# Griffin-style block with 64 experts on one core: the experts' sums kept with channels on partitions, and a narrower overlap of the two half groups

## The reference, cut to what matters

```python
s = sigmoid(xt @ router_w)                      # 512 x 64
idx = top_k(s + router_bias, 6)                 # 6 experts of 64 for each token
w = s[idx] / sum(s[idx]) * 2.5
y = sum over the 6 of w_e * ((silu(xt @ gate_e) * (xt @ up_e)) @ down_e)   # 1024 -> 256 -> 1024
y = y + ((silu(xt @ ws_gate) * (xt @ ws_up)) @ ws_down)                    # shared expert
out = layer_norm(2 ** 0.25 * xt + y) * g + b
```

## Time and profile before

| what | before |
|---|---|
| time of the profiled execution | 1144.19 us |
| its span, first to last instruction | 1142.2 us |
| median of three runs | 1144.53 us |
| TensorE busy (PE) | 1109.3 us, 97% |
| VectorE busy (DVE) | 723.1 us, 63% |
| ScalarE busy (ACT) | 445.4 us, 39% |
| GpSimd busy (POOL) | 210.3 us, 18% |
| read from HBM over the span | 287.62 MB |
| mean granted TensorE clock | 0.997 |

### The profile page before, as it was taken

One profiled execution on the slowest core, in us unless ns is written; L12 is line 12 of the kernel. 1 busy time (PEld: TensorE's weight loads), 2 busy tenths in 40 slices (PEclk: granted clock), 3 DMA queues, 4 the chain that ended last, 5 costly groups with the idle time before them and its releaser, 6 DMA issues.

```text
span 1142.2 us, 19416 instructions
## 1 busy us (share of the span) xinstructions
PE 1109.3 (97%) x7184; PEld 690.4 (60%) x7184; DVE 723.1 (63%) x1298; ACT 445.4 (39%) x696; POOL 210.3 (18%) x117
## 2 busy tenths in 40 slices
PE   5999999999999999999989999999999999999996
PEld 4889888888888888656534444444444444444443
DVE  7868585858585868685634555555555555555556
ACT  6766665766666656402002112221121122212214
POOL 1443333424243424400010000000000000000000
PEclk9999999999999999999999999999999999999998
DMA  6121212122121303149389999999999999999971
GB/s 241 43 111 42 112 44 110 55 101 78 75 95 60 119 35 134 51 174 376 142 343 419 419 420 421 420 420 419 420 420 420 417 416 416 409 419 415 410 319 78
DMA packets 48323, 286.70 MB, mean 251 GB/s; under 512 B 8994, under 2 KB 10530, under 8 KB 16528
## 3 DMA queue, kind: packets, MB, share of 16 engines
q1 hardware_dynamic: 43088, 272.96, 58.8%
q0 software_dynamic: 5184, 12.98, 2.9%
HBM read 287.62 MB, written 4.19 MB: 255 GB/s over the span
## 4 chain that ended last, share of the span: by engine, by line
PE 52%; DVE 2%; ACT 1%; DMA 1%; issue 0%; POOLq 0%; DVEq 0%
PE pair L1441 22%; PE pair L1504 11%; PE pair L1494 9%; PE pair L935 3%; PE pair L1104 2%; PE pair L186 1%; PE pair L188 1%; DMA xg<-h_rows,idx 1%; PE pair L1452 1%; DVE acc L1648 0%; ACT first L1570 0%; PE pair L1097 0%; DVE table L1326 0%; PE pair L898 0%; PE pair L1118 0%
## 5 line engine op out<-in xcount | busy, mean ns | idle before, releaser
L395 PE MATMUL pair<-hT,w_parts 128*128 128x264 f32 (+1 forms) x2112 | 378.5, 338 | 0.9 <-DVE hT L666 0.5
L395 PEld LDWEIGHTS pair<-hT,w_parts 128*128 128x128 f32 x2112 | 319.7, 189 | 46.5 <-issue 3.8
L242 POOL TENSOR_TENSOR w_parts<-w_raw,w_parts 128x1024 fp32r<-128x1024 f32 x66 | 163.5, 2479 | 295.5 <-ACT w_parts L236 282.1
L1593 DVE TENSOR_TENSOR acc<-acc,pair 128x512 f32<-128x512 f32 x272 | 165.6, 681 | 38.6 <-PE pair L1494 38.6
L1441 PE MATMUL pair<-raw,xgT 128*64 128x512 f32 x768 | 170.3, 595 | 0.1
L927 POOL DMA_INDIRECT xg<-h_rows,idx x36 | 35.9, 997 | 529.9 <-DVE idx L921 461.3
L1441 PEld LDWEIGHTS pair<-raw,xgT 128*64 128x64 f32 x768 | 53.2, 137 | 116.2 <-issue 116.2
L1553 ACT ACTIVATE y_hi<-pair,small 128x512 fp32r<-128x512 f32 x70 | 48.2, 688 | 192.0 <-PE pair L1504 192.0
L1584 DVE TENSOR_TENSOR act_a<-act_s,pair 128x256 f32<-128x256 f32 x35 | 14.8, 422 | 167.9 <-ACT act_s L1546 167.9
L1546 ACT ACTIVATE act_s<-pair 128x256 f32<-128x256 f32 x35 | 13.4, 384 | 224.7 <-PE pair L1441 224.7
L1504 PE MATMUL pair<-raw,aT 128*32 128x512 f32 x768 | 87.4, 595 | 0.0
(11 more groups left out here) (302 smaller groups left out, 1335.0 us busy)
## 6 DMA issues: line engine op xcount, KB each, us to landing
raw<-in_w_gate_up SPq DMA_DIRECT2D x96, 1024.0 KB
raw<-in_w_down SPq DMA_DIRECT2D x48, 1024.0 KB
first<-in_w_gate_up SPq DMA_DIRECT2D x44, 1024.0 KB
w_raw<-in_w_in SPq DMA_DIRECT2D x36, 1024.0 KB, 6.6
first<-in_w_down SPq DMA_DIRECT2D x22, 1024.0 KB
xin<-in_x SPq DMA_DIRECT2D x4, 512.0 KB, 5.5
ws_gu<-in_ws_gate_up SPq DMA_DIRECT2D x1, 2048.0 KB, 7.6
h_rows<-acc SPq DMA_DIRECT2D x4, 512.0 KB, 20.2
```

What stands on the lines that cost most here:

```text
L242: pool.tensor_tensor(w[:, n % PARTS, 1], w_raw[:, n // 2, n % 2], w[:, n % PARTS, 0].bitcast(F32), ALU.subtract).then_inc(sem("w_lo_ready" ...
L395: last = pe.matmul(o, w[:, n % PARTS, pw, k * P:(k + 1) * P], hT[ph][:, k, of], start=(k == 0 and m == 0), stop=(k == KB - 1 and m == 2))
L1593: v.tensor_tensor(part, part, SUM[g], ALU.add).then_inc(sem("sum_free"), 1)
```

## The change

The sums are kept turned, as `accT`: channels on partitions (channel 8c + k in plane k), 512 tokens along a row. It lies where `acc` lay.

- Scatter: for each of eight channel planes the weights are 128 channels of y (every eighth) and ST's columns move: 288 for the low slots (tokens 0 to 287), 288 for the high slots (tokens 224 to 511). Low slots of one plane and high slots of the next run side by side, then the other way round. The rule for items follows: tokens under 288 may stand low, tokens from 224 high. EXTRA is 90, so tables have 154 items.
- The look-up of pair p + 3 goes ahead of the scatter, on TensorE and on VectorE. `down` waits for the first two additions.
- The routing's 0/1 tables (`ones_b`, `before_b`, `chosen`) are bf16; the table keeps three columns of weights, and the two columns of token numbers are written once into the three buffers `table_now`.
- The shared expert's down product makes the turned result (weights `ws_dn` at a stride of eight) in eight steps; the residual is taken from `h1T`.
- SPq: the first gate-up chunks of third 2 are issued last, behind `shared_taken`, since they lie over `h1T`.
- End: eight products with the identity turn each tile back, y moves with a stride of eight, VectorE reads PSUM with a stride of 128 and writes rows into `raw`.

The diff, cut to its core:

```diff
-EXTRA = 2 * P * TOP_K // HALF + (T - 2 * P) * TOP_K // SLOTS
+LOW_END, HIGH_AT = 288, 224
+EXTRA = 2 * HIGH_AT * TOP_K // HALF + (LOW_END - HIGH_AT) * TOP_K // SLOTS
...
-DOWN_BANK = (4, 2, 6, 4)
+DOWN_BANK = (4, 5, 2, 3, 6, 7, 4, 5)
...
-        self.SUM = tuple(banks[n] for n in (4, 5, 6, 7, 1, 2, 3, 0))
+        self.SUM = tuple(banks[n] for n in (4, 5, 1, 7, 6, 2, 3, 0))
...
         sp.wait_ge(sem("shared_up_done"), 4)
+        bring(2, 1, 2)
+        sp.wait_ge(sem("shared_done"), KB)
+        bring(2, 0, 2)
+        sp.wait_ge(sem("shared_taken"), KB)
         for u in range(PAIR):
             bring(2, u, 0)
-        bring(2, 1, 2)
-        sp.wait_ge(sem("shared_done"), TT)
-        bring(2, 0, 2)
...
-            for n in range(2):
-                for j in range(2):
-                    last = pe.matmul(banks[DOWN_BANK[t] + n][:, :], aT[:, j, t * P:(t + 1) * P],
-                                     ws_dn[:, j, n * 512:(n + 1) * 512], start=(j == 0), stop=(j == 1))
+            for j in range(2):
+                last = pe.matmul(banks[DOWN_BANK[k]][:, :], ws_dn[:, j, k::KB], aT[:, j], start=(j == 0), stop=(j == 1))
...
+        pe.wait_ge(sem("pool_step"), BF16_READY)
         for n, of in numbers:
-            for t in of:
-                last = pe.matmul(TOT[:, n * E:(n + 1) * E], ones[:], chosen[:, t, 0], start=(t == of[0]), stop=(t == of[-1]))
+            for t, rows in of:
+                last = pe.matmul(TOT[:, n * E:(n + 1) * E], ones_b[rows], chosen[rows, t, 0], start=(t == 0),
+                                 stop=(t == of[-1][0]))
...
         for m in range(2):
-            st.add(v.tensor_copy(table[:, 0:ITEMS, :, 3 + m],
-                                 tok[:, :, m].rearrange("p (i t) -> p i t", i=1).broadcast_to([P, ITEMS, TT])))
+            st.add(v.tensor_copy(pairs.all_now[:, :, :, :, PARTS_W + m].rearrange("p b u t -> p (b u) t"),
+                                 tok[:, :, m].rearrange("p (i t) -> p i t", i=1).broadcast_to([P, THIRDS * PAIR, TT])))
...
-        for t in range(TT):
-            v.wait_ge(sem("shared_done"), t + 1)
-            v.scalar_tensor_tensor(acc[:, t], acc[:, t], ALPHA, pair[DOWN_BANK[t] // 2][:, :], ALU.mult, ALU.add)\
+        for k in range(KB):
+            v.wait_ge(sem("shared_done"), k + 1)
+            v.scalar_tensor_tensor(accT[:, k], h1T[:, k], ALPHA, banks[DOWN_BANK[k]][:, :], ALU.mult, ALU.add)\
              .then_inc(sem("shared_taken"), 1)
...
+    SIDES = ((LOW, slice(0, LOW_END)), (HIGH, slice(HIGH_AT, T)))
...
+                for k in range(KB):
...
+                    pe.matmul(o[k // 4][:, k % 4 * P:(k % 4 + 1) * P], accT[:, k, rows], ident[:], start=(k % 4 == 0),
+                              stop=False, skip_group_check=True)
...
+                        last = pe.matmul(o[m].rearrange("p (k c) -> p k c", k=KB // 2), ST[b][:, rows],
+                                         part[:].rearrange("p (c k) -> p k c", k=KB)[:, m * KB // 2:(m + 1) * KB // 2],
+                                         start=False, stop=(part is y_lo), skip_group_check=True)
...
+            def add_in(g, turn):
+                for part in (y_hi, y_lo):
+                    for i in range(2):
+                        of, cols = SIDES[(turn + i) % 2]
+                        last = pe.matmul(SUM[g + i][:, cols], part[of, g + i::KB], ST[b][of, cols],
+                                         start=(turn == 0 and part is y_hi), stop=(turn == 1 and part is y_lo),
+                                         skip_group_check=True)
+                return last
+
+            def first_half(g):
                 if g == SHARED:
 
+                    pe.wait_ge(sem("look_free"), p + THIRDS + 1)
                     pe.wait_ge(sem("xgT_ready"), 2 * p + 4)
...
                 if g == LAST:
 
                     pe.wait_ge(sem("aT_ready"), p + 1)
...
+                add_in(g, 0).then_inc(sem("half_done"), 1)
+
+            def second_half(g):
+
+                pe.wait_ge(sem("half_done"), HALVES * p - HALVES + g // 2 + 1)
+                add_in(g, 1).then_inc(sem("sum_done"), 2)
+
+            first_half(0)
+            first_half(2)
+            second_half(0)
+            first_half(4)
+            second_half(2)
+            first_half(6)
+            second_half(4)
+            second_half(6)
...
             turn_a(p)
+            pairs.look_up(pe, p + 3, b)
             scatter(p, (b + 2) % THIRDS)
 
-            pe.wait_ge(sem("sum_free"), ADDS * p + LOOK_AT + 1)
-            pairs.look_up(pe, p + 3, b)
+            pe.wait_ge(sem("sum_free"), ADDS * p + 2)
 
             down(p, b, turn)
...
-            part = acc[:, t, m * 512:(m + 1) * 512]
-            v.tensor_tensor(part, part, SUM[g], ALU.add).then_inc(sem("sum_free"), 1)
+            v.tensor_tensor(accT[:, g], accT[:, g], SUM[g], ALU.add).then_inc(sem("sum_free"), 1)
...
             weigh(p, b)
+            look(p, b)
             add_up(p)
-            look_and_part(p, b)
+            part_y(p)
...
-                rows = acc[:, TILES[t], part]
-                st(v.scalar_tensor_tensor(rows, LAST_AT[t][:, part], neg_mean[:, col], g2[:, part], ALU.add, ALU.mult))
+                rows, of_c = done[t][:, part], slice(part.start // KB, part.stop // KB)
+                st(v.scalar_tensor_tensor(by_k(rows), LAST_AT[t][:, :].rearrange("p (k c) -> p c k", k=KB)[:, of_c],
+                                          neg_mean[:, col], by_k(g2[:, part]), ALU.add, ALU.mult))
```

More of the change, by code:

```diff
@@ L145, in program @@
         mem["ones"] = sb("ones", [P, P])
+        mem["acc_at"] = top[0]
         mem["acc"] = sb("acc", [P, TT, D])
+        mem["accT"] = sb("accT", [P, KB, T], at=mem["acc_at"])
         raw_at = top[0]
@@ L844, in __init__ @@
         thirds = range(THIRDS)
[L846 removed]
+        now = self.all_now = mem["table_now"]
         self.table_now = [now[:, b] for b in thirds]
@@ L924, in gather @@
         pool.wait_ge(self.sem("idx_ready"), p + 1)
-        pool.sem_inc(self.sem("gather_begun"), 1)
+        pool.sem_inc(self.sem("pool_step"), 1)
         pool.wait_ge(self.sem("h1_stored"), 16 * TT)
@@ L953, in out_and_route @@
     ident, ones, acc, merged, raw = (mem[n] for n in ("ident", "ones", "acc", "merged", "raw"))
-    h1_rows, table, slot_of, iota = (mem[n] for n in ("h1_rows", "table", "slot_of", "iota"))
+    h1_rows, table, slot_of, iota, accT = (mem[n] for n in ("h1_rows", "table", "slot_of", "iota", "accT"))
     place = top[0]
@@ L1026, in out_and_route @@
     TOT = banks[1][:, TT * E:(TT + 3) * E]
-    numbers = ((0, (0, 1, 2)), (1, (TT - 1,)), (2, (0,)))
+    numbers = [(n, [(t, slice(0, min(P, end - P * t))) for t in range(TT) if end > P * t])
+               for n, end in enumerate((LOW_END, T, HIGH_AT))]
     ROW = 2 * ITEMS
@@ L1359, in _ @@
         pool.wait_ge(sem("pool_step"), 2 * PAIR + 1)
+        pool.memset(ones_b[:], 1.0).then_inc(sem("pool_step"), 1)
+        pool.wait_ge(sem("pool_step"), 2 * PAIR + 2)
+        pool.wait_ge(sem("route_here"), 16 * 9)
+        pool.tensor_copy(before_b[:], before[:]).then_inc(sem("pool_step"), 1)
+        pool.wait_ge(sem("pool_step"), BF16_READY)
         pool.wait_ge(sem("shared_up_done"), 4)
@@ L1392, in experts @@
     parts = lambda t: (slice(0, D),) if t < TT - 1 else (slice(0, D // 2), slice(D // 2, D))
+    by_k = lambda row: row.rearrange("p (c k) -> p c k", k=KB)
+    done = [mem["raw"][:, t // 2, t % 2 * D:(t % 2 + 1) * D] for t in range(TT)]
     @block.sync
@@ L1421, in _ @@
                 sp.wait_ge(sem("out_ready"), i + 1 + (part.start > 0))
-                sp.dma_start(out[t * P:(t + 1) * P, part], acc[:, t, part]).then_inc(sem("stored"), 16)
+                sp.dma_start(out[t * P:(t + 1) * P, part], done[t][:, part]).then_inc(sem("stored"), 16)
         sp.wait_ge(sem("stored"), 16 * (TT + 1))
@@ L1461, in finish @@
             pe.wait_ge(sem("xgT_ready"), 2 * p + 2)
-            for i, t in enumerate(TILES):
-                o = [LAST_AT[i][:, m * 512:(m + 1) * 512] for m in range(2)]
-                for m in range(2):
-                    if i == TT - 1 and m == 0:
+            for t in TILES:
+                o = [LAST_AT[t][:, m * 512:(m + 1) * 512] for m in range(2)]
+                rows = slice(t * P, (t + 1) * P)
+                for k in range(KB):
+                    if t == TT - 1 and k == 0:
                         pe.wait_ge(sem("y_ready"), 2 * p)
-                    pe.matmul(o[m], ident[:], acc[:, t, m * 512:(m + 1) * 512], start=True, stop=False)
-                if i == 0:
+                    pe.matmul(o[k // 4][:, k % 4 * P:(k % 4 + 1) * P], accT[:, k, rows], ident[:], start=(k % 4 == 0),
+                              stop=False, skip_group_check=True)
+                if t == 0:
                     pe.wait_ge(sem("ST_ready"), p)
@@ L1480, in scatter @@
             pe.wait_ge(sem("y_ready"), 2 * p)
-            for g in range(0, ADDS, 2):
-                now = SUMS[g:g + 2]
+            def add_in(g, turn):
```

(16 more changed lines are left out.)

81 lines of the change are left out of this document (44 added, 37 removed).

## The result

The changed kernel takes **1175.78 us** (median of four runs, 1174.22 to 1176.94) against 1144.76 for the kernel before beside it: ratio **1.0275**, interval 1.0251 to 1.0298. It is 31 us slower. The forecast was 1145.5 in a range of 1139 to 1154; the result lies where the first rival, "slower, by strides", put it: 1175 us at a chance of 8%.

The account below looks back on a forecast made before the run. TensorE and the DMA stream were taken to end together in the experts' stage. Pair 34 -1.7, scatter and order -0.4, tail +2.9 and +0.5 sum to +1.3 us on 1144.19: 1145.5 us, range 1139 to 1154.

Parts of the forecast that it names:

- the first rival: Scatter weight loads slow at a stride of eight words, +0.85 us for each of 34 pairs: 1175 us, chance 8%.
- The step that failed: Scatter on TensorE: 16 steps at 0.133 us plus 0.3 for switching array tiling, 2.4 us, nothing added for strides.
- The bound that stood in the same paragraph: Upper end for the scatter: 3.9 us if the strided weight loads ran at half their rate.
- All three signs of being wrong: Scatter over 3.1 us, gate-up never waiting for a weight, or last VectorE passes still at 1.28 us.
- The two bounds: Experts' stage: TensorE at 15.23 us a pair and the DMA stream at 16.0 to 16.3 end together; 0.5 us room.
- The stream's start: Third pair's first chunks are issued later, behind the last shared addition, so the DMA stream is delayed: +1.9 us.
- The gathers: Over 32 gathers the fullest block of eight slots has 249 rows, not 256: -1.0 us on the DMA stream.
- The routing and the first gather: Before the pairs: cheaper bf16 routing instructions, -1.4 us; shorter TensorE wait for the first gather, -0.7 us.
- The tail: Last normalization: VectorE's strided PSUM pass at 2.0 us a tile, +2.9; TensorE's products moving strided y, +0.5 us.
- the penalty for a new line of PSUM: Skill's rule cited for the stride rival: accesses each falling in a new 8-byte line of PSUM run slower.
- The rival that it doesn't do what it says: Scatter's half-height products of different columns not running side by side, 16 steps becoming 32; counted with the first rival.
- The rival of a faster kernel, where the stream is no bound: Experts' stage: DMA engines have room, so TensorE's 10 us and the start's 2 come through: 1135 us, chance 6%.

Follow-up runs that it names:

- Half loads: Only half the columns of each down chunk loaded from pair 3 on: in the contiguous version 1127.48 us, in the kernel before 1144.42 us.
- the contiguous version: Changed kernel with the experts' down-weight columns laid out in eight planes of 128, so y is read without a stride: 1146.15 us, ratio 0.9999.

## Why the prediction was wrong, and where it was right

**The step that failed** is the scatter's: "The nearest row for these is the turning of x, which loads weights of that same stride and takes 1.17 us for eight, 0.146 each with its start; so nothing is added." It made 2.4 us; measured 4.09. The row was that of transposes, whose loads are of another kind, and no contiguous row was set beside it to tell whether the stride cost anything in it; the same trace had one (L1452, 140 ns for 195). So the remark that these rows "do not show it for weight loads" was a misreading too. The bound that stood in the same paragraph, 3.9 us for loads at half their rate, was the right one, and the rival's condition (a step over 0.17 us) was met with 0.241. All three signs of being wrong that the prediction names came: a scatter over 3.1 us, a gate-up that never waits for a weight, and VectorE's last passes still at 1.28 us. The rival's own sum, +0.85 us a pair and 1175 us, was right to 0.05 and 1 us; only its chance was wrong.

**The two bounds** were read rightly. Half loads show that the kernel before has 0.44 us from the stream, for which the prediction took 0.5. In the contiguous version, which has the loads that the prediction assumed, the forecast's picture comes out: a step of 0.131 for 0.133, a period of 14.74 for 14.9, set by the additions "by a hair", the stream taking over at pair 20 for "about pair 25", and 1146.15 us for 1145.5. Part of that agreement is luck, as the next terms show.

**The stream's start**: +1.9 us. From the first chunk's issue to pair 34 the contiguous version takes 533.6 us (573.21 to 1106.85) and the kernel before 531.9 (573.73 to 1105.64): +1.7. The DMA share falls at 574 to 590, 0.76 for 0.95; from 587 to 590 it is 0.31, where no traffic was forecast.

**The gathers**: -1.0 us, from blocks of eight slots. Wrong: by the pattern that the runs bear out the fullest engine goes from 252 rows to 251, so about nothing. The price of a row, 0.15 us in the term, was near the 0.13 measured.

**The routing and the first gather**: -1.4 and -0.7. Pair 0 starts 1.9 us earlier after the mixer's end than before, for 2.1. The 28 small products take 1.2 us (545.06 to 546.22), for 1.4; TensorE waits 1.88 us for the table, for 0.71 before, and 0.97 for the gather, for 1.43.

**The tail**: +2.9 from VectorE and +0.5 from TensorE, behind -0.4 from the scatter and the order: +3.0 together. Measured +2.5, and the nearness is luck. Of it, 0.9 is the slow scatter in front of the last down products, and the tail proper, from the first product of the identity to the end, takes 22.9 us (1152.12 to 1175.05) for 21.4 (1120.87 to 1142.23): +1.6 in place of +3.4, none of it from VectorE's pass. VectorE first, then TensorE, in the changed kernel:

```profile
1162.60 1.28 DVE L1695 SCALAR_TENSOR_TENSOR raw<-pair,first 128x1024 f32<-128x1024 f32 x1
...
1166.11 1.28 DVE L1695 SCALAR_TENSOR_TENSOR raw<-pair,first 128x1024 f32<-128x1024 f32 x1
```

```profile
1161.42 0.62 PE L1501 MATMUL pair<-y_lo,ST 128*128 128x512 f32 x1
1161.85 0.62 PE L1501 MATMUL pair<-y_hi,ST 128*128 128x512 f32 x1
```

VectorE's pass reads PSUM at a stride of 128 words in the same 1.28 us as without, so the penalty for a new line of PSUM, which the prediction names, does not show in it. The moving products of TensorE are what slows: one each 0.43 us, for 0.23 in the contiguous version, so that a tile takes 3.51 us for 3.27, and the first one 0.85 more. They were given 0.6 us of cover in the later tiles, which four products at 0.2 more use up. The contiguous version's tail proper takes 21.4 us as before, which shows the rest of the new tail to cost nothing.

**The rival that it doesn't do what it says**: excluded. Two half-height products of different columns run side by side in 0.131 us. The rival of a faster kernel, where the stream is no bound, is excluded by the half-load runs. Without the strides, in fact, the stream decides from pair 20 on.

## What to carry to other kernels

Before a change turns a contiguous loaded operand into a strided one, look for two rows of the *same kind* of instruction, one strided and one not; a row of a neighbouring kind shows a price but not what the stride added. A layout of the weights in memory can take such a stride away for nothing. And where two bounds end together, a gain on one is worth what the other allows: it took the stream's fullest engine, not its bytes, to bring the change below the kernel before.

## What was not expected of the hardware

A load of 128 fp32 columns takes 185 to 191 ns contiguously, 193 at a stride of two words, 327 at four, 335 at eight. A moving product of 512 columns slows from 391 to 645 ns at a stride of only two, and no further at four or eight (656, and 618 to 644 ns). VectorE reads PSUM at a stride of 128 words at no cost (1.28 us for 1024 elements). A transpose loads in 141 ns where a product of the same shape takes 191 and two instructions. Skipped rows of a gather leave some DMA engines short of work by over a hundred rows, and numbering the slots so that they spread is worth 3.9 us here.
